# Other places in the plan of a hybrid decoder layer: norms, recurrence, cache loads of the samples and dense steps

## The chip, the cores and the metric

The kernel runs on one core of a Trainium2 chip. The metric is the device time of one execution in microseconds (us), shorter is better. The core has five instruction queues that are in order each and wait for one another by semaphores: TensorE (PE; its weight loads are PEld), VectorE (DVE), ScalarE (ACT), GpSimd (POOL) and SyncE (SP), which here issues all DMA transfers.

## What is computed

One layer of a decoder on 2048 prompt tokens and on 64 sample tokens (8 sequences of 8), cut to what matters here:

```
h = rmsnorm(x)
z = h @ W_in      # q, k, v, indexer q/k/w, GLA q/k/v/r, gate
A = sparse attention: score[t,s] = sum_h w[t,h] * relu(iq[t,h] . ik[s]);
    each query keeps its 256 best keys; softmax(q.k / 8 + bias) over those; @ v
G = gated linear attention in chunks of 64 (a recurrence over the prompt), norm, swish gate
x = x + concat(A, G) @ W_out
x = x + W_down(silu(W_gate h2) * (W_up h2)),  h2 = rmsnorm(x)
y = rmsnorm(x)
```

The samples do the same against a paged cache of 512 keys each and keep 130 keys. The 256 best keys are found by rounds: MAX8 gives the eight largest of a row, MATCH_REPLACE8 takes them out, and 32 rounds make 256 (17 rounds for the samples).

## The kernel before

The prompt goes through in 8 blocks of 256 tokens. Tokens stand in columns, features in partitions. Every dense product takes its weights as two fp16 halves (high and low) and the activations too, and runs three matmuls (L763, L764, L765) in place of one.

The order of the work on all five queues is one list, `PLAN` (function `plan`). Each engine goes through the whole list and does its own part of every step, so a step's place in the list is its place in every queue. For block b the list holds, between three kinds of places:

- **The head of block b**, from the barrier before `PR` to the next: `PR` (norm of the input), the output products `O` of block b-1, `YS` and `YR` (square and scale of the final norm of block b-2, then its store), `XF` (load of the residual of block b-1 and its sum with the `O` products), the 13 input products `P` of block b (25 in block 0), and between these, as the tables `E_NARROW` and `E_WIDE` say (the number is the `P` step behind which a step stands), the index key norm and the gates (`E1` to `E5`), the recurrence (`GA`, `GC`, `GD1`, `GD2`), and `FS` and `FR` (square and scale of the second norm of block b-1). Then the first `HEAD_USES` steps `U` (gate and up products of block b-1), then a barrier.
- **The attention of block b**: index scores `I`, 32 picking rounds `K` for the first 128 queries, `KE`, the rounds for the second 128 queries, and 16 units `A` (2 x 8 heads: logits, softmax, transposes, values). The rest of the `U` steps and the first six of the eight `D` (down products, 66 matmuls each) of block b-1 are spread over this by `interleaved`: it gives each attention step a weight and puts a dense step wherever the share of dense weight done falls behind the share of attention weight passed. The weights are estimates written in `attention_steps`.
- In block 1 the samples' own attention stands ahead of that: `IS0` (which also issues the cache loads), eight `IS` (index scores), 17 rounds `KS`, eight `AS`.

A `U` step of a narrow block holds two weight tiles of 128x1024 and 48 matmuls of 256 columns; the 320-column blocks (b = 1 for `U` and `D`, b = 0 for `P`) have one tile a step.

**Weights.** Six ring slots hold the split tiles. In the first two blocks that use a tile, it is loaded raw, and ACT (`highs`, L1137) and DVE (`lows`, L1429) split it; one of the two blocks writes the halves back to DRAM (L642), and later blocks load them ready (L635). Within a step these stand ahead of the step's own work, and on SP the loads follow the list too:

```
if kind in ("P", "O", "U", "D"):          # SP
    for n in tiles_in(at):
        if n + 5 < len(TILE):
            load(n + 5)
def highs_ahead(at):                      # ACT; DVE's lows_ahead is alike
    for n in tiles_in(at):
        for m in range(5) if n == 0 else [n + 4]:
            if m < len(TILE):
                highs(m)
```

So SP is five tiles ahead of the step that TensorE is to do, and ACT and DVE four. `SP` waits at `YR` for DVE's `y_done` before it stores y (L743), and at the samples' `IS0` for the barrier before it issues one load for the indicator rows, 32 for the index keys (L648), one for the bias, and 12 for keys and values; each of the 44 reads a page number from SBUF first. All dense steps alternate between two PSUM banks, which are released by the evacuation by ACT (`gr`, `gk`, `gq`, `gv`, `v`, `O`, `U`, `D`) or by DVE (`k`, `iq`, `q`, L1565 to L1584).

Of the kernel before, what the change touches and what calls it, by code (L numbers as in the profile page):

```python
# [144 lines left out]
def o_uses(b):  # L145
    return [[t] for t in range(KT)] if b == 1 else [[t, t + 1] for t in range(0, KT, 2)]
# [7 lines left out]
def tiles_of(b):  # L154
    return (2 * b, 2 * b + 1)


E_NARROW = {1: ["E1"], 2: ["E2", "FS"], 3: ["E3", "FR"], 4: ["E4"], 5: ["E5"], 6: ["GA"], 7: ["GC0"], 8: ["GC1", "OUTP"],
            10: ["GD1"], 12: ["GD2"]}
E_WIDE = {3: ["E1"], 5: ["E2"], 6: ["E3"], 9: ["E4"], 10: ["E5"], 11: ["GA"], 12: ["GC0"], 13: ["GC1", "OUTP"],  # L160
          14: ["GSA"], 15: ["GSB"], 16: ["GSN0", "GSN1"], 17: ["GSN2", "GSN3"], 18: ["GSN4", "GSN5"],
          19: ["GSN6", "GSN7"], 22: ["GD1"], 24: ["GD2"]}
HEAD_USES = 4
D_TAIL = 2


def attention_steps(b):

    out = []
    if b == 1:  # L170
        out.append((("IS0", b), 3.0))
        out += [(("IS", b, s), 1.0) for s in range(DB)]
        out.append((("IS9", b), 1.0))
        out += [(("KS", b, r), 1.3) for r in range(ROUNDS_S)]
        out.append((("AS0", b), 2.0))
        out += [(("AS", b, s), 3.0) for s in range(DB)]
        out.append((("AS9", b), 1.0))
        out.append((("BAR", b), 0.5))
    i0, i1 = tiles_of(b)

    def pick(i, r):
        return ("K", b, i, r), 2 * 128 * (i + 1) / 960.0 + 0.3

    def unit(i):
        keys = 128 * (i + 1)
        return max(0.3, keys * 1.6e-3 + 1.2 - keys * 0.84e-3 - (i + 1) * 0.22)

    if b:
# [4 lines left out]
        out.append((("KE", b, i0), 0.5))  # L193
        late = [pick(i1, r) for r in range(ROUNDS)]
    else:
# [40 lines left out]
def plan():  # L236
    steps = [("START", 0), ("PQ", 0)]
    for b in range(NBLK):
# [5 lines left out]
        if b:  # L244
            steps += [("O", b - 1, k) for k in range(len(o_uses(b - 1)))]
            if b >= 2:
                steps += [("YS", b - 2), ("YR", b - 2)]
            steps.append(("XF", b - 1))
# [131 lines left out]
def layer(nc, a):  # L380
    with ExitStack() as ctx:
# [226 lines left out]
        def _(sp):  # L608
# [42 lines left out]
            for at, step in enumerate(PLAN):  # L651
# [38 lines left out]
                if kind == "XF":  # L690
                    if b == 0:
                        for who in ENG:
                            sp.wait_ge(S("bar_" + who), BARS[at - 2 - len(o_uses(0))] + 1)
                    else:
                        sp.wait_ge(S("y_done"), b)
# [22 lines left out]
                if kind == "GD1" and b == NBLK - 1:  # L718
                    sp.wait_ge(S("g_state"), 4 * NBLK)
                    sp.dma_start(a["o_gp"], state[:, :, :]).then_inc(S("outputs"), 16)  # L720
                    outs += 16
                if kind == "IS0":
                    for who in ENG:
# [1323 lines left out]
```

## Time and profile before

| what | value |
|---|---|
| median of 3 runs | 4444.63 us (4441.96 to 4448.02) |
| the profiled execution's own time | 4443.38 us |
| its span, first to last instruction | 4441.6 us |
| PE busy | 3334.8 us, 75% |
| DVE busy | 2531.8 us, 57% |
| ACT busy | 1192.0 us, 27% |
| POOL busy | 1077.5 us, 24% |
| DMA queue q1 | 509.88 MB, 35.3% of 16 engines |
| chain that ended last | PE 29%, DVE 19%, issue 18%, DVE's sequencer 15% |

No engine is busy throughout. Three quarters for TensorE is an average over stages with different limits, so the profile has to be read stage by stage: the head of a block, and its attention. Times in a timeline are counted from the start of the span. PEclk is the share of the full TensorE clock that was granted.

### The profile page before, as it was taken

To read this page: it belongs to the slowest core of one execution; us is meant where nothing else is said; L and a number is where in the kernel's file an instruction comes from. 1 tells how busy PE (TensorE), PEld (TensorE's weight loads), DVE (VectorE), ACT (ScalarE), POOL (GpSimd) and SP (SyncE) were. 2 spreads that over 40 slices of the span, in tenths; PEclk is the share of its full clock that TensorE was granted. 3 is DMA by queue.
4 is the path that set the end of the run, shared out by engine and by line. 5 is a ranking of instruction groups with operands and counts; after the bars stand their busy time and mean duration, and the time that the engine had idled before them with its cause. 6 is when DMAs were issued, how large, how long until landed. Compare 5 with 4: busy or idle time off the path is not lost.

```text
span 4441.6 us, 67462 instructions
## 1 busy us (share of the span) xinstructions
PE 3334.8 (75%) x26714; PEld 2689.3 (61%) x26714; DVE 2531.8 (57%) x4016; ACT 1192.0 (27%) x2002; POOL 1077.5 (24%) x979
## 2 busy tenths in 40 slices
PE   6867477778987878888677957879657889167687
PEld 3656245666666767676566646666546676156577
DVE  3537158645852397238953498534997247996100
ACT  2334123333323221323132301333112324012211
POOL 0233113123612332133112222122310123010142
PEclk8978678789998989999798978889878899678889
DMA  4335344344634433243214332143312143011244
GB/s 155 117 126 186 100 129 144 119 154 137 230 127 140 131 122 125 96 150 125 78 56 152 113 105 85 49 148 108 124 59 66 62 165 125 32 60 52 86 148 147
DMA packets 200573, 514.20 MB, mean 116 GB/s; under 512 B 20242, under 2 KB 79458, under 8 KB 200130
## 3 DMA queue, kind: packets, MB, share of 16 engines
q1 hardware_dynamic: 200258, 509.88, 35.3%
q8 instruction: 212, 3.47, 0.3%
q14 instruction: 103, 0.84, 0.1%
HBM read 443.67 MB, written 66.15 MB: 115 GB/s over the span
## 4 chain that ended last, share of the span: by engine, by line
PE 29%; DVE 19%; issue 18%; DVEq 15%; POOLq 7%; ACT 4%; POOL 3%; DMA 2%; SPq 1%; ACTq 0%
DVEq L1442 11%; DVE top L1439 10%; PE bank L763 6%; PE bank L764 6%; PE bank L765 6%; PE bank L812 3%; DVE T L1462 2%; ACT T L1362 2%; DVEq L1440 2%; PE bank L801 1%; POOLq L1793 1%; DMA FR<-in_xT 1%; DVE T L1441 1%; DVE ring L1429 1%; PE bank L788 1%
## 5 line engine op out<-in xcount | busy, mean ns | idle before, releaser
L763 PE MATMUL bank<-FR,ring 128*128 128x256 f16 (+1 forms) x4224 | 1199.2, 284 | 42.5 <-DVE ring L1429 23.9
L764 PE MATMUL bank<-FR,ring 128*128 128x256 f16 (+1 forms) x4224 | 1197.5, 284 | 0.0
L765 PE MATMUL bank<-FR,ring 128*128 128x256 f16 (+1 forms) x4224 | 1195.3, 283 | 0.0
L1439 DVE MAX8 top<-T 128x8 f32<-128x384 f32 (+14 forms) x465 | 651.7, 1402 | 34.0 <-POOL T L1933 4.2
L1441 DVE MATCH_REPLACE8 T<-top,T 128x384 f32<-128x384 f32 (+14 forms) x465 | 644.2, 1385 | 1.2 <-issue 1.2
L788 PE MATMUL bank<-kT,q 128*128 128x256 f16 (+3 forms) x384 | 134.7, 353 | 513.4 <-DVE mx L1462 489.6
L763 PEld LDWEIGHTS bank<-FR,ring 128*128 128x128 f16 x4224 | 428.6, 101 | 121.8 <-issue 20.0
L764 PEld LDWEIGHTS bank<-FR,ring 128*128 128x128 f16 x4224 | 425.2, 101 | 74.5 <-issue 1.7
L765 PEld LDWEIGHTS bank<-FR,ring 128*128 128x128 f16 x4224 | 425.1, 101 | 73.8
L788 PEld LDWEIGHTS bank<-kT,q 128*128 128x128 f16 x384 | 44.0, 115 | 588.8 <-DVE mx L1462 552.6
L763 PE MATMUL bank<-T,ring 128*128 128x256 f16 (+3 forms) x1280 | 372.9, 291 | 35.0 <-DMA ring<-halves_kept 17.5
L812 PE MATMUL bank<-vtok,T 128*128 128x64 f32 x2176 | 341.4, 306 | 75.6 <-DVE T L1475 56.6
L1462 DVE CUSTOM_DVE_ANT_0 T<-bank,T 128x256 f32<-128x256 f32 (+3 forms) x384 | 194.0, 534 | 339.3 <-PE bank L790 238.9
L812 PEld LDWEIGHTS bank<-vtok,T 128*128 128x128 f32 x2176 | 326.5, 227 | 95.9 <-issue 53.8
L764 PE MATMUL bank<-T,ring 128*128 128x256 f16 (+3 forms) x1280 | 371.6, 290 | 0.0
L765 PE MATMUL bank<-T,ring 128*128 128x256 f16 (+3 forms) x1280 | 370.3, 289 | 0.0
L1409 DVE TENSOR_TENSOR T<-T 128x256 f32<-128x256 f32 (+1 forms) x32 | 13.8, 432 | 606.7 <-ACT T L1121 606.7
L1159 ACT ACTIVATE T<-bank 128x512 f32<-128x512 f32 (+3 forms) x320 | 165.1, 528 | 423.5 <-PE bank L801 423.4
L1150 ACT ACTIVATE T<-T,nmax 128x128 f32<-128x128 f32 (+15 forms) x128 | 153.1, 1196 | 439.0 <-DVE nmax L1465 439.0
L1910 POOL TENSOR_TENSOR ev<-ev 128x512 f32<-128x512 f32 (+1 forms) x99 | 121.9, 1231 | 451.3 <-ACT ev L1336 448.5
L801 PE MATMUL bank<-cst,T 128*128 128x128 f32 x1088 | 205.3, 313 | 18.5 <-ACT T L1150 18.4
L1905 POOL TENSOR_TENSOR ev<-ev 128x512 f32<-128x512 f32 (+1 forms) x99 | 121.5, 1227 | 367.7 <-ACT ev L1334 367.1
(285 smaller groups left out, 5622.4 us busy)
## 6 DMA issues: line engine op xcount, KB each, us to landing
ring<-halves_kept SPq DMA_DIRECT2D x605, 512.0 KB, 3.5
halves_kept<-ring SPq DMA_DIRECT2D x93, 512.0 KB, 5.1
ring<-halves_kept SPq DMA_DIRECT2D x52, 384.0 KB, 3.4
kT<-in_w_gu SPq DMA_DIRECT2D x33, 512.0 KB, 6.1
kT<-in_w_in SPq DMA_DIRECT2D x18, 512.0 KB, 6.7
ikT<-in_w_gu SPq DMA_DIRECT2D x17, 512.0 KB, 5.9
T<-in_xT SPq DMA_DIRECT2D x8, 1024.0 KB, 6.8
FR<-in_xT SPq DMA_DIRECT2D x8, 1024.0 KB, 8.4
```

What stands on the lines that cost most here:

```text
L763: mm(o, lhs[0], rhs[0], start=first, stop=False)
L764: mm(o, lhs[0], rhs[1], start=False, stop=False)
L765: return mm(o, lhs[1], rhs[0], start=False, stop=last)
L788: mm(bank[2 + n % 2][:, 0:kn], q[:, h, cq:cq + 128], kT[:, h // 4, 0, k0:k0 + kn], start=True, stop=False)
L801: last = nc.tensor.transpose(bank[4 + n % 2][:, 128 * (t % 4):128 * (t % 4) + 128], lg[:, u % 2, 128 * t:128 * t + 128], ident)
L812: last = mm(bank[6 + u % 2][:, 0:64], pT[:, GN[i, h, g] % 3, t % 4, :], vtok[:, t, e:e + 64], start=(t == 0), stop=(t == i))
L1150: A(lg[:, u % 2, 0:128 * (i + 1)], lg[:, u % 2, 0:128 * (i + 1)], ACT.Exp, bias=nmax[:, u % 2:u % 2 + 1], accum_out=den[:, u % 4:u % 4 + 1 ...
L1159: A(pT[:, m % 3, 0:w, :], bank[4 + n % 2][:, 0:128 * w].rearrange("p (t n) -> p t n", n=128), ACT.Copy).then_inc(S("a_pTc"), 1)
L1439: v.max(top8[rows, :], view)
L1441: v.match_replace(view, top8[rows, :], view, TAKEN)
L1442: dve.drain()
L1462: v.tensor_tensor_reduce(lg[:, u % 2, k0:k0 + kn], bank[2 + n % 2][:, 0:kn], m, 1.0 / Q_SCALE, OUTSIDE, ALU.add, ALU.max, mx[:, u % 2, c:c ...
```

## The change

It moves steps in the list and adds one step, `LOADS`, which has only SP's part of the former `IS0`. No arithmetic and no transfer is added or taken away.

```
-E_NARROW = {1: ["E1"], 2: ["E2", "FS"], 3: ["E3", "FR"], 4: ["E4"], 5: ["E5"], 6: ["GA"], 7: ["GC0"], 8: ["GC1", "OUTP"],
-            10: ["GD1"], 12: ["GD2"]}
+E_NARROW = {1: ["E1"], 2: ["E2"], 3: ["E3", "FS"], 4: ["E4"], 5: ["E5", "FR"], 8: ["GA"], 9: ["GC0"], 10: ["GC1", "OUTP"],
+            11: ["GD1"], 12: ["GD2"]}
-E_WIDE = {3: ["E1"], 5: ["E2"], 6: ["E3"], 9: ["E4"], 10: ["E5"], 11: ["GA"], ...
+E_WIDE = {3: ["E1"], 5: ["E2"], 7: ["E3"], 9: ["E4"], 11: ["E5"], 13: ["GA"], ...
...
-HEAD_USES = 4
+HEAD_USES = 6
...
-        out.append((("IS0", b), 3.0))
-        out += [(("IS", b, s), 1.0) for s in range(DB)]
+        out.append((("LOADS", b), 60.0))
+        out.append((("IS0", b), 5.0))
+        out += [(("IS", b, s), 1.5) for s in range(DB)]
...
-        out += [(("AS", b, s), 3.0) for s in range(DB)]
+        out += [(("AS", b, s), 5.0) for s in range(DB)]
...
-        return max(0.3, keys * 1.6e-3 + 1.2 - keys * 0.84e-3 - (i + 1) * 0.22)
+        return max(0.3, 2.5 - keys * 1e-3)
...
-        late = [pick(i1, r) for r in range(ROUNDS)]
+        late = [(step, w - 0.4) for step, w in (pick(i1, r) for r in range(ROUNDS))]
...
-            steps += [("O", b - 1, k) for k in range(len(o_uses(b - 1)))]
+            uses = [("O", b - 1, k) for k in range(len(o_uses(b - 1)))]
+            half = len(uses) // 2
             if b >= 2:
-                steps += [("YS", b - 2), ("YR", b - 2)]
+                steps += [("YS", b - 2)] + uses[:half] + [("YR", b - 2)] + uses[half:]
+            else:
+                steps += uses
...
-                if kind == "IS0":
+                if kind == "LOADS":
```

In `E_WIDE`, `GD1` goes from 22 to 23, the recurrence of the samples by two places, and `GD2` stays at 24. The `XF` wait of block 0 is written by another index and names the same barrier. Four lines come in ahead of the engines' code, so that a line of the code before stands four lines further down now (L1348 is L1352).

The list itself changes in this way (narrow blocks, b of 3 to 7): `PR O O O O YS YR XF P...` becomes `PR YS O O YR O O XF P...`; `FS` stands one and `FR` two `P` steps later, `GA` and `GC` two, `GD1` one. Two `U` steps leave the attention for the head. In block 1, four `U` steps stand in the attention ahead of the index scores of the prompt that were behind them: before, 1 `U` step stood between the barrier and `IS` 0 and 11 between the barrier and the end of the samples' part; now 7 and 14, of which six stand between `LOADS` and `IS0`. In the attention of blocks 1 to 4 the last spread `D` steps move behind the last picking round: one in blocks 1, 3 and 4, two in block 2. In blocks 5 to 7 they stay ahead of it.

**ACT in the first instructions behind the barrier of block 1's samples.** L1333 and L1334, L1336 are the evacuations of a `U` pair, L1137 the high halves of the tiles ahead, L1366 `IS0`, L1372 and L1373 `IS`. Before:

```order
L1366 ACTIVATE T<-bank 64x512
L1137 ACTIVATE ring<-ikT 128x1024
L1137 ACTIVATE ring<-kT 128x1024
L1333 ACTIVATE ev<-bank 128x512
L1334 ACTIVATE ev<-bank 128x512
L1372 ACTIVATE T<-bank 64x512
L1373 ACTIVATE T<-bank 64x64
```

The same place now (L1141 is the high half, L1337 and L1338, L1340 the evacuations, L1370 `IS0`), from the fourth `U` step behind `LOADS` on:

```order
L1141 ACTIVATE ring<-kT 128x1024
L1141 ACTIVATE ring<-vtok 128x1024
L1340 ACTIVATE ev<-bank 128x512
L1141 ACTIVATE ring<-ikT 128x1024
L1141 ACTIVATE ring<-kT 128x1024
L1337 ACTIVATE ev<-bank 128x512
L1338 ACTIVATE ev<-bank 128x512
L1141 ACTIVATE ring<-kT 128x1024
L1141 ACTIVATE ring<-vtok 128x1024
L1340 ACTIVATE ev<-bank 128x512
L1370 ACTIVATE T<-bank 64x512
L1141 ACTIVATE ring<-ikT 128x1024
```

`IS0` stood ahead of the first `U` step and stands behind six of them now, with their twelve splits.

**DVE in the head of block 6.** L1524 to L1531 are `FR`, L1409 to L1415 a Newton step of a norm, L1615 to L1625 `E4`, L1637 and L1638 `E5`, L1565 the evacuation of the seventh `P` step. Before:

```order
L1524 SCALAR_TENSOR_TENSOR FR<-FR,gvec,T 128x256 x4
L1529 CAST FR<-FR 128x1024
L1531 TENSOR_TENSOR FR<-FR 128x1024
L1409 TENSOR_TENSOR T<-T 128x256
L1411 TENSOR_TENSOR T<-T 128x256
L1413 TENSOR_SCALAR T<-T 128x256
L1415 TENSOR_TENSOR T<-T 128x256
L1615 TENSOR_TENSOR T<-T 128x256
L1619 TENSOR_SCALAR ik<-T,gates 128x256
L1623 TENSOR_SCALAR ikT<-ik 128x256
L1625 SCALAR_TENSOR_TENSOR ikT<-ik,ikT 128x256
L1637 TENSOR_TENSOR T<-T 64x2x256
```

The same queue now, from the end of `E5` on:

```order
L1642 TENSOR_TENSOR T<-T 64x2x256
L1413 TENSOR_TENSOR T<-T 128x256
L1415 TENSOR_TENSOR T<-T 128x256
L1417 TENSOR_SCALAR T<-T 128x256
L1419 TENSOR_TENSOR T<-T 128x256
L1528 SCALAR_TENSOR_TENSOR FR<-FR,gvec,T 128x256 x4
L1533 CAST FR<-FR 128x1024
L1535 TENSOR_TENSOR FR<-FR 128x1024
L1528 SCALAR_TENSOR_TENSOR FR<-FR,gvec,T 128x256 x4
L1533 CAST FR<-FR 128x1024
L1535 TENSOR_TENSOR FR<-FR 128x1024
L1569 TENSOR_SCALAR k<-bank 128x512
```

`FR` stood ahead of `E4` and `E5`; now it stands behind both and directly ahead of the evacuation of the seventh `P` step.

## Rows read from the trace of the kernel before

**Rows 1.** Busy time by stretch: stretch, length, busy (count) by engine, PEclk, DMA.

```profile
451.00:679.00 228.00, 141.43 (x905) 93.17 (x906) 82.67 (x156) 47.71 (x89) 31.18 (x27) 0.71 0.38 118
679.00:892.00 213.00, 156.57 (x1137) 128.24 (x1136) 159.04 (x358) 72.67 (x126) 55.95 (x53) 0.82 0.41 134
...
1068.00:1374.00 306.00, 272.45 (x1889) 198.53 (x1889) 199.31 (x368) 101.24 (x202) 113.63 (x133) 0.93 0.46 156
...
2908.00:3072.00 164.00, 136.19 (x1274) 118.18 (x1274) 58.14 (x103) 46.04 (x66) 49.28 (x36) 0.91 0.45 150
3072.00:3513.00 441.00, 313.40 (x2304) 245.78 (x2304) 341.27 (x434) 113.45 (x203) 75.30 (x78) 0.84 0.22 71
```

**Rows 2.** Waits of TensorE, head of block 6 (2908:3072): total, times, longest us.

```profile
PE bank L780 <- POOL FR L1791: 9.7, 2, 7.2
PE bank L929 <- DVE T L1638: 9.3, 1, 9.3
...
PE bank L763 <- DMA ring<-halves_kept: 1.3, 1, 1.3
```

**Rows 3.** Timeline of GpSimd, same head: start, length, instruction, idle before.

```profile
2932.32 4.62 POOL L1791 TENSOR_TENSOR FR<-FR 128x1024 f32<-128x1024 f32 x3 [21.63 <-ACT FR L1348]
```

**Rows 4.** Timeline of SP, same head: the store of y.

```profile
2947.49 0.59 SPq L743 DMA_DIRECT2D o_y<-FR  x1
```

**Rows 5.** Timeline of VectorE, same head: begin of `FR`, begin of `E4`.

```profile
2974.07 0.43 DVE L1409 TENSOR_TENSOR T<-T 128x256 f32<-128x256 f32 x1 [9.42 <-ACT T L1121]
...
2983.28 0.42 DVE L1409 TENSOR_TENSOR T<-T 128x256 f32<-128x256 f32 x1
```

**Rows 6.** Timeline of GpSimd, same head: begin of `GD2`, of two `U` pairs.

```profile
3042.61 1.89 POOL L1779 TENSOR_TENSOR T<-T 128x1024 f32<-128x1024 f32 x1 [47.58 <-ACT T L1304]
...
3059.89 1.27 POOL L1905 TENSOR_TENSOR ev<-ev 128x512 f32<-128x512 f32 x1
...
3065.97 1.27 POOL L1905 TENSOR_TENSOR ev<-ev 128x512 f32<-128x512 f32 x1
```

**Rows 7.** Timeline of ScalarE, same head: an evacuation of a `U` step.

```profile
3062.65 0.60 ACT L1333 ACTIVATE ev<-bank 128x512 f32<-128x512 f32 x1 [4.64 <-PE bank L765]
```

**Rows 8.** Waits of TensorE, head of block 2 (892:1068).

```profile
PE bank L1045 <- POOLq L562: 12.3, 1, 12.3
PE bank L929 <- DVE T L1638: 11.0, 1, 11.0
PE bank L780 <- POOL FR L1791: 10.0, 2, 7.0
PE bank L763 <- DMA ring<-halves_kept: 4.5, 1, 4.5
```

**Rows 9.** Timeline of SP behind the barrier of block 1.

```profile
450.75 0.51 SPq L726 DMA_DIRECT2D T<-in_rep  x1
...
490.14 12.43 SPq L648 DMA_DIRECT2D T<-in_cache  x12
```

**Rows 10.** Timeline of ScalarE, its first row behind those loads.

```profile
507.70 1.06 ACT L1137 ACTIVATE ring<-kT 128x1024 f16<-128x1024 f32 x1 [49.24 <-DMA kT<-in_w_gu]
```

**Rows 11.** Timeline of VectorE: first round `KS`, first split behind it.

```profile
541.85 0.76 DVE L1439 MAX8 top<-T 64x8 f32<-64x582 f32 x1 [0.82 <-ACT T L1376]
...
554.80 1.23 DVE L1429 SCALAR_TENSOR_TENSOR ring<-kT,ring 128x1024 f16<-128x1024 f32 x1 [10.00 <-ACT ring L1137]
```

**Rows 12.** Timeline of GpSimd, head of block 1: beside VectorE's splits, and without.

```profile
436.56 2.06 POOL L1907 TENSOR_TENSOR ev<-ev 128x512 f32<-128x512 f32 x1
...
445.83 1.26 POOL L1907 TENSOR_TENSOR ev<-ev 128x512 f32<-128x512 f32 x1
```

**Rows 13.** Groups of VectorE, block 1's picking (679:832): busy us, mean ns.

```profile
L1429 DVE SCALAR_TENSOR_TENSOR ring<-vtok,ring 128x1024 f16<-128x1024 f32 (+1 forms) x7 | 10.4, 1485 | 0.1
```

**Rows 14.** Waits of TensorE, block 0 (80:240).

```profile
PE bank L922 <- DVE T L1593: 8.2, 1, 8.2
PE bank L929 <- DVE FR L1638: 5.1, 1, 5.1
```

More of the change, by code:

```diff
@@ L155, in tiles_of @@
     return (2 * b, 2 * b + 1)
-E_NARROW = {1: ["E1"], 2: ["E2", "FS"], 3: ["E3", "FR"], 4: ["E4"], 5: ["E5"], 6: ["GA"], 7: ["GC0"], 8: ["GC1", "OUTP"],
-            10: ["GD1"], 12: ["GD2"]}
-E_WIDE = {3: ["E1"], 5: ["E2"], 6: ["E3"], 9: ["E4"], 10: ["E5"], 11: ["GA"], 12: ["GC0"], 13: ["GC1", "OUTP"],
-          14: ["GSA"], 15: ["GSB"], 16: ["GSN0", "GSN1"], 17: ["GSN2", "GSN3"], 18: ["GSN4", "GSN5"],
-          19: ["GSN6", "GSN7"], 22: ["GD1"], 24: ["GD2"]}
-HEAD_USES = 4
+E_NARROW = {1: ["E1"], 2: ["E2"], 3: ["E3", "FS"], 4: ["E4"], 5: ["E5", "FR"], 8: ["GA"], 9: ["GC0"], 10: ["GC1", "OUTP"],
+            11: ["GD1"], 12: ["GD2"]}
+E_WIDE = {3: ["E1"], 5: ["E2"], 7: ["E3"], 9: ["E4"], 11: ["E5"], 13: ["GA"], 14: ["GC0"], 15: ["GC1", "OUTP"],
+          16: ["GSA"], 17: ["GSB"], 18: ["GSN0", "GSN1"], 19: ["GSN2", "GSN3"], 20: ["GSN4", "GSN5"],
+          21: ["GSN6", "GSN7"], 23: ["GD1"], 24: ["GD2"]}
+HEAD_USES = 6
 D_TAIL = 2
@@ L692, in _ @@
                         for who in ENG:
-                            sp.wait_ge(S("bar_" + who), BARS[at - 2 - len(o_uses(0))] + 1)
+                            sp.wait_ge(S("bar_" + who), BARS[AT["PR", 1] - 1] + 1)
                     else:
```

## The prediction, made before the changed kernel was run

> **What bounds the kernel now.** The page first: TensorE is busy 75% of the span, VectorE 57%, and the chain that ended last has shares of both, so there is no single bound. The view by stretches divides it [rows 1]. In the head of a block (164 us in block 6) TensorE is busy 136 us, VectorE 58: TensorE sets the pace, and 28 us are waits. In the attention from block 3 on VectorE is the bound: 341 of 441 us in block 6, most of it picking, with TensorE's dense steps lying beside it. Block 2's attention has the wide dense steps and is TensorE's: 272 of 306 us. Block 1 is neither: in the samples' part (451 to 679) nobody is busy over 62%, in the prompt's part (679 to 892) VectorE is at 159 of 213 us, because it splits raw weights as well as picking.
>
> The waits of TensorE in a head come next [rows 2, 8]. Three go to the norms: `YR`'s sum (7.2 us in block 6), the weights held back by SP's wait for y (1.3 here, 4.5 in block 2), `FR`'s sum (9.7 less 7.2, so 2.5). The fourth is `GA`, 9.3 and 11.0 us, waiting for `E5` on VectorE, which stood behind `FR`. A head ends on GpSimd: `GD2` starts at 3042.61, the two `U` pairs at 3059.89 and 3065.97 [rows 6], so a pair costs 6.1 us and the barrier opens at 3072.1. In block 2 TensorE waits 12.3 us for that [rows 8]. A `U` step costs TensorE 5.2 us (4.64 us of waiting plus 0.60 of evacuation) [rows 7]; a narrow `D` step has 66 matmuls against 48, so 7.2.
>
> All durations are of the profiled execution, 4443.4 us in all (span 4441.6); the median is 1.2 us more.
>
> **Heads of blocks 2 to 7.** I follow block 6, whose head begins at 2908. `YS` now stands ahead of the `O` steps. ScalarE is free 5 us in, squares for 2 us (the sum on GpSimd started 21.6 us after its last work, because ScalarE first had to evacuate four `O` steps), the sum takes 4.6 us alone [rows 3] and would be done 11.5 us in, when two `O` steps of 5.3 us have just ended. But VectorE now scales the input (`PR`) at that very time. Beside VectorE's splits a GpSimd add took 2.06 us in place of 1.26 [rows 12]; at that ratio the sum takes 7.6 us. So `YR`'s wait is between 0 and 3.5 us; I take 1.5. y is stored 10.6 us after its sum (the sum at 2936.9, the store at 2947.49 [rows 3, 4]), so about 24 us in, against 39 now. SP waits there, and has loaded only up to the first half of the first `P` step. TensorE arrives at the second half about 29 us in and the tile lands behind 1 MB of y: a wait of 1 to 5 us, I take 2.6 (before, 1.3). `FR`'s sum comes one `P` step later: 1.8 us left of 2.5. `GA`'s wait goes whole, since `E4` and `E5` are no longer behind `FR`. In its place: `FR` takes VectorE 9.2 us [rows 5] directly ahead of the evacuation of the seventh `P` step, which frees the bank of the ninth. I get 4.3 us of a new wait there, bounds 0 and 9.2. Sum: old waits 20.3, new 10.2, and 2.6 us less at the half clock behind the long wait: 12.7 us won at `GA`. Of this `GD1` gives back one `P` step, 5.2, since it stands behind the twelfth now; and the barrier one more pair on GpSimd, 6.1 us, as three `U` pairs follow `GD2` instead of two. Left: 1.4 us, with two more `U` steps done. So the waits go, and the tail takes nearly all. By the same steps blocks 4 and 7 give 2, block 6 2, blocks 3 and 5 (longer waits before) 5 each. Block 2: 25.5 us of waits besides the barrier [rows 8], new ones some 10, clock 5, so 21 won, 5.2 and 4.4 (a narrower pair) given back: 11. Heads together: 27 us less. Bounds 5 and 45: each of the six can be 3 us off on either side.
>
> The Trainium skill, page "SBUF — State Buffer", section "SBUF: two separate sides", says that VectorE and GpSimd share a port pair as an exclusive lock, so that the loser blocks for the whole instruction. The two GpSimd rows agree in direction, 2.06 against 1.26 us [rows 12]. By the lock the moved sum could last its own 4.6 us plus all of `PR`'s 7.4, done 19 us in, and `YR`'s wait would be the old one; the six heads would then give some 30 us less.
>
> **The two `U` steps that leave the attention.** From block 3 on they lay beside picking on VectorE and cost nothing there, so nothing comes back: value 0, bounds 0 and 2 a block. In block 2 TensorE is the bound, so two wide steps (3.3 us each) come back, and two `D` steps fill a wait behind the last picking round: 9.5 us less. Block 3's last `U` among the index scores moves behind them: 1.5 less.
>
> **`D` steps behind the last round.** In blocks 3 and 4 one `D` (7.2 us) moves from under the picking, where TensorE had room, into the last units, where TensorE is the bound. Two times 6.7 us more, 3 us back because the logits of the units before are less late: 10.5 more. Bounds 3 and 15.
>
> **Block 0.** `E3` one step later takes 4 of its 8.2 us wait, the later `GA` all 5.1 [rows 14]; `GD1` stands one step later, 3.4 us. 6 us less, bounds 0 and 10.
>
> **Block 1.** This is the largest term, and it goes the other way.
> Head: its waits go as above, but VectorE's splits run beside GpSimd to the end, so a third `U` pair takes 8 to 10 us, and the head ends 9 us later.
> Samples: SP issues the 44 cache loads from 450.75 to 502.6 [rows 9], and no weight meanwhile. In the kernel before ScalarE got its next raw tile at 507.70, after 49.2 us of waiting [rows 10], and TensorE could do one `U` step ahead of that. Now six `U` steps stand between `LOADS` and `IS0`, but SP's queue still has all 44 loads ahead of the third one's weights. So TensorE does two (10.5 us), waits some 46 us, and only then does the other four, 5.3 us each at least; then `IS0` must go through GpSimd, VectorE and ScalarE with TensorE idle for 8 to 12 us, then `IS` with two `U` steps among them. The first round `KS` stood 91 us behind the barrier (541.85 [rows 11]); I get 133. `KS` then has two `U` steps among it in place of four and loses part of the 10 us wait for a split [rows 11]: 32 us for 51. `AS` is the same but for its last `U` step. So the samples' part ends 20 us later, with three more `U` steps done.
> Prompt: five fewer dense steps, 13 fewer splits at 1.4 us [rows 13], so 18 us off VectorE, and 5 of its waits; a `U` step now stands among the index scores (5.5 more) and a `D` with its splits behind the last round (8 more). 10 us less.
> Block 1 together: 19 us more. Bounds: 5 less (everything that leaves the prompt's part comes back at its pace there, 10 us a step, for half the steps) and 45 more (nothing comes back, and the four steps run at 7.8 us).
>
> **Sum.** -27 (heads) -9.5 (block 2) -1.5 (block 3) +10.5 (`D`) -6 (block 0) +19 (block 1) = -14.5 us: 4428.9 for the profiled execution, 4430 beside the median. `KS`, `K` and the products are the same instructions; the last block's end is untouched.
>
> **Rivals.**
> (a) Block 1 gives its time back. The prompt's part is bound by VectorE's splits and picking; if `U` steps there cost what they seem to, 10 us each, five fewer make up for the samples, and the total is -35 to -45: 4400. For it: VectorE at 159 of 213 us [rows 1]. Against it: the rounds stay, only the splits go.
> (b) The heads give nothing. GpSimd ends each head with three pairs in place of two, and if its sums are slowed as by the lock above, blocks 3 to 7 are level and block 2 gives 5: -27 becomes -5, the sum +7.5, so 4452 at the far end, 4443 if half of it. For it: the barrier already waited for GpSimd in every head [rows 6, 8]. Against it: at least 12 us of waits per head go first.
> (c) Slower: the queue of SP in block 1. The six `U` steps behind `LOADS` are starved by the 44 loads; the price is the stretch from barrier to `KS`, and it decides from 45 us (the 43.5 of the heads, block 2 and 0, less the `D` steps' 10.5, plus the 9 that can be told). At 50 us of loss in block 1 the total is +17: 4461. For it: 49.2 us of waiting for a raw tile [rows 10], which no step of the change shortens. Against it: work done before need not be done later.
> (d) That nothing happens, because all is off the path: +-5 us. Against it the barrier waits above. Counted with (b).
>
> **Chances.** Forecast (4415 to 4437) 0.45; (a) 0.17; (b) and (d) 0.20; (c) 0.18. About 0.2%, 9 us, is what a measurement of this kernel can tell from no change. Below 4435.7: (a), most of the forecast, 0.57. Within: 0.26. Above 4453.5: 0.17. Range: 4400 to 4462, from (a) to (c).
>
> **What would show it.** In the heads TensorE's wait at `GA` is gone, one of 2 to 6 us is there at the ninth `P` step, and three `U` pairs stand behind `GD2` on GpSimd. In block 1 TensorE waits over 40 us for a raw tile within 15 us of the barrier, `IS0`'s first matmul comes some 90 us behind it, and the prompt's part is about 10 us shorter. The prediction is wrong if `GA` still waits, if the heads end over 6 us earlier each, or if the samples' part is no longer than before.

## The result, and the profile after

The changed kernel takes 4491.36 us (median of 4 runs, 4488.87 to 4514.35) against 4443.3 us (median of 4, 4438.3 to 4448.02): ratio 1.012, interval 1.0085 to 1.0155. It is slower by 48 us where 4430 was predicted. The profiled execution has a span of 4490.3 us, 48.7 more than before.

The same stretches as in [rows 1], read from the changed kernel (stretch, length, busy time and count by engine, PEclk, DMA): head and samples' part of block 1; its prompt's part; head of block 2; attention of blocks 2, 3 and 4; head and attention of block 6.

```profile
270.90:699.30 428.40, 294.19 (x2416) 230.06 (x2416) 196.45 (x285) 129.03 (x194) 108.21 (x75) 0.81 0.49 157
699.30:903.20 203.90, 125.48 (x896) 101.60 (x896) 142.72 (x348) 59.93 (x109) 32.20 (x37) 0.76 0.28 94
903.20:1071.10 167.90, 136.04 (x1227) 110.00 (x1228) 77.44 (x109) 53.00 (x79) 55.92 (x45) 0.93 0.50 167
1071.10:1386.10 315.00, 272.49 (x1840) 195.59 (x1841) 199.70 (x368) 99.41 (x199) 109.81 (x128) 0.91 0.46 151
1557.40:1859.90 302.50, 233.49 (x1824) 193.19 (x1824) 205.30 (x370) 72.69 (x136) 69.20 (x72) 0.87 0.30 97
2028.80:2384.50 355.70, 262.14 (x1953) 210.57 (x1953) 251.31 (x386) 86.56 (x168) 69.49 (x73) 0.85 0.26 82
2944.60:3114.20 169.60, 143.17 (x1370) 124.65 (x1371) 63.58 (x103) 47.30 (x69) 54.06 (x41) 0.94 0.48 157
3114.20:3557.20 443.00, 295.08 (x2208) 231.12 (x2209) 341.33 (x434) 112.25 (x200) 69.75 (x72) 0.83 0.21 66
```

The same stages of the kernel before, for the comparison (block 1 in its two parts, attention of block 4):

```profile
280.50:678.90 398.40, 276.01 (x2177) 209.66 (x2178) 184.84 (x275) 114.66 (x177) 86.26 (x60) 0.79 0.45 146
678.90:891.80 212.90, 156.47 (x1137) 128.13 (x1137) 159.04 (x358) 72.67 (x126) 55.76 (x53) 0.82 0.41 133
2000.50:2344.50 344.00, 260.89 (x2048) 211.06 (x2048) 251.71 (x386) 88.35 (x171) 75.42 (x77) 0.90 0.29 91
```

Block 1's first part is 30 us longer, its second 9 shorter. The head of block 6 has 96 matmuls more than before (two `U` steps) and is 5.4 us longer; the attention behind it has 96 fewer and is 2.3 us longer. Stage by stage (attention of block 7 without its last two `D` steps, which both kernels have):

| stages | before | after | difference | predicted |
|---|---|---|---|---|
| block 0 | 262.3 | 252.9 | -9.4 | -6 |
| block 1 | 611.3 | 632.3 | +21.0 | +19 |
| heads of blocks 2 to 7 | 1004.9 | 1015.0 | +10.1 | -27 |
| attention of block 2 | 305.8 | 315.0 | +9.2 | -9.5 |
| attention of blocks 3 and 4 | 637.4 | 658.2 | +20.8 | +9 |
| attention of blocks 5 to 7 | 1311.9 | 1309.0 | -2.9 | 0 |

Where the head's time went is in its waits. Waits of TensorE in the head of block 6 of the changed kernel (engine, line, what it waited for: us, times, longest):

```profile
PE bank L767 <- DVE kT L1574: 7.9, 1, 7.9
PE bank L767 <- DMA ring<-halves_kept: 6.2, 1, 6.2
...
PE bank L1012 <- ACT T L1296: 1.8, 1, 1.8
PE bank L784 <- POOL FR L1795: 1.7, 2, 1.4
```

Against [rows 2]: `GA` no longer waits, `YR`'s sum 0.3 us, `FS`'s 1.4. The wait for the weights behind y is 6.2 us where it was 1.3, and a new one of 7.9 stands at the ninth `P` step. With the 0.3, the 1.4 and the 1.8 at `GD1` these are 17.6 us, where 20.3 stood before. In both long waits the moved sums have a part, which VectorE's and GpSimd's timelines show together. VectorE at the scaling of the input (`PR`, L1513), then at the begin of `E4` (L1619 and L1623):

```profile
2951.51 5.18 DVE L1513 SCALAR_TENSOR_TENSOR T<-T,gvec 128x256 f32<-128x256 f32 x4
...
2958.68 1.67 DVE L1513 SCALAR_TENSOR_TENSOR T<-T,gvec 128x256 f32<-128x256 f32 x4
...
3004.95 2.61 DVE L1619 TENSOR_TENSOR T<-T 128x256 f32<-128x256 f32 x1
3007.64 1.20 DVE L1623 TENSOR_SCALAR ik<-T,gates 128x256 f32<-128x256 f32 x1
```

GpSimd, the sum of `YS` in the same head:

```profile
2951.39 4.62 POOL L1795 TENSOR_TENSOR FR<-FR 128x1024 f32<-128x1024 f32 x3 [4.26 <-ACT FR L1352]
```

And the first of these rows of `E4` in the kernel before, where no sum lay beside it:

```profile
2985.14 0.42 DVE L1615 TENSOR_TENSOR T<-T 128x256 f32<-128x256 f32 x1
2985.64 0.41 DVE L1619 TENSOR_SCALAR ik<-T,gates 128x256 f32<-128x256 f32 x1
```

Four scalings take 5.18 us while GpSimd's sum runs and 1.67 when it is over; an addition of 0.42 us takes 2.61 beside `FS`'s sum. GpSimd keeps its 4.62 us. So these moved sums were not slowed, as I had taken; they hold VectorE up by 3.5 us each. `E4` goes on in `L1627` and `L1629` to 3010.20, so 5.25 us in all for 1.80 before. All six heads have both holds: the four scalings take 5.2 to 6.2 us for 1.7, `E4` 5.25 to 6.25 for 1.8.

The kernel before had the same already. In the head of block 1, beside the GpSimd addition of [rows 12] that took 2.06 us for 1.26, VectorE's split takes 2.29 us, where one alone takes 1.23 [rows 11]. In the head of block 6 `E5`'s second addition takes 1.74 us beside one of GpSimd, its first 0.68:

```profile
435.21 2.29 DVE L1429 SCALAR_TENSOR_TENSOR ring<-ikT,ring 128x1024 f16<-128x1024 f32 x1
...
2989.39 0.68 DVE L1637 TENSOR_TENSOR T<-T 64x512 f32<-64x512 f32 x1 [2.46 <-ACT T L1264]
2990.00 1.74 DVE L1638 TENSOR_TENSOR T<-T 64x512 f32<-64x512 f32 x1
```

The first hold goes on through ScalarE, which needs the scaled tiles' buffer for `YR`'s root. The root begins 4.4 us behind the sum's end, where it was 1.3 before, so 3.1 us are lost there:

```profile
2960.44 0.47 ACT L1121 ACTIVATE T<-bank,cst 128x256 f32<-128x256 f32 x1 [4.04 <-DVE T L1513]
```

So y is stored at 2969.68 (SP's timeline), 25.1 us into the head, and SP, which had issued three weight tiles ahead of it, issues the next at 2970.39. TensorE has waited for that tile since 26.6 us into the head when it lands (last row, PE's timeline):

```profile
2947.94 5.56 SPq L639 DMA_DIRECT2D ring<-halves_kept  x3
2969.68 0.59 SPq L747 DMA_DIRECT2D o_y<-FR  x1
2970.39 3.55 SPq L639 DMA_DIRECT2D ring<-halves_kept  x4
...
2977.47 0.39 PE L767 MATMUL bank<-T,ring 128*128 128x256 f16 x1 [6.22 <-DMA ring<-halves_kept]
```

Then the end of the head, on GpSimd: the Newton steps behind `GD1`, and three `U` pairs behind `GD2`.

```profile
3078.36 1.90 POOL L1783 TENSOR_TENSOR T<-T 128x1024 f32<-128x1024 f32 x1 [60.04 <-ACT T L1308]
...
3095.62 1.27 POOL L1909 TENSOR_TENSOR ev<-ev 128x512 f32<-128x512 f32 x1
...
3101.71 1.27 POOL L1909 TENSOR_TENSOR ev<-ev 128x512 f32<-128x512 f32 x1
...
3107.80 1.26 POOL L1909 TENSOR_TENSOR ev<-ev 128x512 f32<-128x512 f32 x1
```

The chain starts 133.8 us into the head; in [rows 6] it started 134.4 us in (3042.61 less 2908.2). All that the norms' move won is 0.6 us there, and the third pair takes 6.1: together the 5.4 us that the head is longer, to 0.1.

In block 1 the prediction's picture came out as drawn. ScalarE behind the barrier:

```profile
452.89 1.06 ACT L1141 ACTIVATE ring<-ikT 128x1024 f16<-128x1024 f32 x1 [8.39 <-POOLq L566]
509.92 1.06 ACT L1141 ACTIVATE ring<-kT 128x1024 f16<-128x1024 f32 x1 [55.98 <-DMA kT<-in_w_gu]
```

ScalarE waits 55.98 us for a raw tile and TensorE 47.1 us for ScalarE (TensorE's waits from 452 to 560):

```profile
PE bank L767 <- ACT ev L1338: 47.1, 1, 47.1
PE bank L767 <- POOLq L566: 13.1, 1, 13.1
PE bank L1055 <- DVE T L1724: 8.5, 1, 8.5
```

The third is `IS0`'s, and `IS0` starts at 544.1, 91 us behind the barrier (90 had been forecast). The block's head is 11.5 us longer, the samples' part 18.5 longer and the prompt's part 9 shorter, for 9, 20 and 10 in the forecast.

### The profile page after: what moved, and what is told of

The parts are those of the page before. It is cut to its first block, busy times and chain, and to the rows that moved or that the text cites. A ratio compares the mean times of both kernels' runs of the same rounds, so it can differ in the third digit from the quotient of the medians.

```text
span 4490.3 us, 67462 instructions
## 1 busy us (share of the span) xinstructions
PE 3320.2 (74%) x26714; PEld 2681.8 (60%) x26714; DVE 2555.9 (57%) x4016; ACT 1191.7 (27%) x2002; POOL 1071.8 (24%) x979
## 4 chain that ended last, share of the span: by engine, by line
PE 33%; DVE 23%; DVEq 17%; issue 11%; POOLq 5%; ACT 5%; POOL 2%; DMA 2%; SPq 1%; ACTq 0%
DVEq L1446 13%; DVE top L1443 11%; PE bank L767 8%; PE bank L768 7%; PE bank L769 7%; PE bank L816 3%; DVEq L1444 2%; DVE T L1466 2%; DVE ring L1433 1%; ACT T L1366 1%; PE bank L805 1%; DVE T L1445 1%; PE bank L792 1%; POOLq L1915 1%; POOLq L1912 1%
## 5 line engine op out<-in xcount | busy, mean ns | idle before, releaser
L767 PE MATMUL bank<-FR,ring 128*128 128x256 f16 (+1 forms) x4224 | 1198.5, 284 | 89.3 <-ACT ev L1338 47.1
L792 PEld LDWEIGHTS bank<-kT,q 128*128 128x128 f16 x384 | 44.1, 115 | 677.1 <-DVE mx L1466 637.4
L1413 DVE TENSOR_TENSOR T<-T 128x256 f32<-128x256 f32 (+1 forms) x32 | 14.9, 466 | 455.2 <-ACT T L1125 455.0
L1923 POOL TENSOR_TENSOR FR<-FR,ev 128x256 f32<-128x256 f32 (+1 forms) x64 | 49.8, 778 | 762.9 <-ACT ev L1349 762.9
L1909 POOL TENSOR_TENSOR ev<-ev 128x512 f32<-128x512 f32 (+1 forms) x99 | 120.6, 1218 | 431.6 <-ACT ev L1338 431.2
```

The lines of the kernel that those rows point to most:

```text
L767: mm(o, lhs[0], rhs[0], start=first, stop=False)
L792: mm(bank[2 + n % 2][:, 0:kn], q[:, h, cq:cq + 128], kT[:, h // 4, 0, k0:k0 + kn], start=True, stop=False)
```

## The experiments

Blocks' times below are from each kernel's own profile, cut at the same steps; medians are of its runs, with the kernel before on the same chip beside them. Each edit is against the changed kernel or against another experiment, as said. The ratios are the recorded ones and not quotients of the two medians. The experiments ran on three chips, on which the kernel before has medians of 4441.81 (e1 to e4), 4439.97 (e5 to e8) and 4444.33 (e9 to e12).

A stretch "from the last round on" is cut at `KE`, the step behind it. How many of the spread `D` steps stand behind the last round decides several experiments, and the list of the steps gives it (before, then changed): 1 and 1 in block 1, 1 and 2 in block 2, 0 and 1 in blocks 3, 4 and 5, none in 6 and 7. So block 2 has one more there, not two, block 1 none, and block 5 has one directly ahead of `KE`. e1 and e9 have 3, 2, 1 and 1 in blocks 2 to 5, and of these one directly ahead of `KE` in blocks 2, 3 and 5.

**Two `U` steps fewer in the heads of blocks 2 to 7.**

```
-            steps += [s for s, _ in u[:HEAD_USES]]
+            steps += [s for s, _ in u[:HEAD_USES.get(b, 4)]]
-HEAD_USES = 6
+HEAD_USES = {1: 6}
```

> The changed kernel with four U steps instead of six between GD2 and the barrier of blocks 2 to 7 (block 1 keeps six); the two that leave go back among the picking rounds. Theory 1 (a head is bound by TensorE and ends on GpSimd, so its last two U steps cost the pair of 6 us there, while among the rounds they lie beside VectorE and are free; and TensorE, having more to do among the rounds, keeps its clock longer): heads 2 to 7 are each 5 to 6 us shorter, attention of blocks 3 to 7 the same or up to 5 us shorter, total 4455 (clock no matter) down to 4440. Rival (work is work: what leaves the head is paid in the attention): attention grows by 5 us a block, total 4485 to 4495.

4476.24 us (before 4441.81; ratio 1.0083, 1.0066 to 1.01). The six heads take 983.8 us for 1015.0, 5.2 each. The attention of blocks 2 to 7 takes 2292.7 for 2282.2: a third of it is paid there. The total lies between the two forecasts: theory 1 for the heads, with a part of the rival behind them. The pair on GpSimd was the price.

**The old weights of rounds and units in blocks 2 to 7.**

```
     def unit(i):
         keys = 128 * (i + 1)
+        if b != 1:
+            return max(0.3, keys * 1.6e-3 + 1.2 - keys * 0.84e-3 - (i + 1) * 0.22)
         return max(0.3, 2.5 - keys * 1e-3)
 ...
-        late = [(step, w - 0.4) for step, w in (pick(i1, r) for r in range(ROUNDS))]
+        late = [(step, w - (0.0 if b != 1 else 0.4)) for step, w in (pick(i1, r) for r in range(ROUNDS))]
```

> The changed kernel with the weights of the picking rounds and units as before for blocks 2 to 7, so that no D step but the last two stands behind the last picking round. Theory 1 (a D step behind the last round costs its full 7 to 9 us in blocks 2, 3 and 4, and is free under the rounds): the tails of blocks 2, 3 and 4 are 7, 8 and 9 us shorter, nothing else moves, total 4467. Rival (the step costs the same under the rounds, since the chain through TensorE's logits is as late there): the stretches under the rounds grow by what the tails lose, total 4485 to 4492.

4503.54 us (before 4441.81; ratio 1.014, 1.0118 to 1.0162), 12 above the change in the medians, which the two intervals don't tell apart. Block 4 does what theory 1 says, from its last round on (the kernel after, then this one):

```profile
2291.70:2384.50 92.80, 75.92 (x553) 62.60 (x553) 22.18 (x88) 31.67 (x59) 14.62 (x18) 0.89 0.18 56
```

```profile
2310.00:2393.10 83.10, 65.54 (x487) 53.80 (x487) 21.70 (x88) 31.18 (x58) 13.93 (x17) 0.92 0.16 51
```

66 matmuls fewer, 9.7 us less. But in block 2, where a `D` step stands between the last round and `KE`, the stretch of the second tile's rounds up to `KE` grows from 121.1 to 135.5 us (to the end of the last round 126.7), and in block 3 from 110.0 to 118.4. VectorE waits 40.3 us there for 27.6 in block 2, of these 33.0 for splits of ScalarE, and 20.8 for 12.4 in block 3, of these 14.9 for logits of TensorE. The attention of blocks 5 to 7, whose weights the edit also changes, is 10 us longer. So theory 1 holds for one block and falls as a sum.

**Block 1 as before** (its norms, four `U` steps in its head, cache loads directly ahead of `IS0`, old weights; `E_ONE` is the old `E_NARROW`).

```
-        out.append((("LOADS", b), 60.0))
-        out.append((("IS0", b), 5.0))
+        out.append((("LOADS", b), 0.0))
+        out.append((("IS0", b), 3.0))
 ...
-        after = E_NARROW if b else E_WIDE
+        after = (E_ONE if b == 1 else E_NARROW) if b else E_WIDE
```

> The changed kernel with block 1 as before: norms of its head, four U steps in it, the cache loads directly ahead of IS0 with the sample steps' old weights, the prompt's picking with the old dense steps. Theory 1 (the six U steps put between the cache loads and IS0 starve behind 44 loads in SP's queue, and only part of the lost time comes back in the prompt's picking): block 1 is 21 us shorter, the rest the same, total 4470. Rival (block 1's loss is the price of moved work, and other blocks change with it, since the clock is granted on what TensorE did before): total 4480 or more, with the heads and block 2 slower by 10 us.

4474.9 us (before 4441.81; ratio 1.0084, 1.0056 to 1.0112). Block 1 takes 611.4 us for 632.3, as before the change (611.3), and every head and attention behind it is within 2 us of the change's. Block 1's 21 us are its own. Its time alone spreads: in the nine traces with the old steps in it, it takes 598.3 to 611.4 us (median 608.9), in the four with the new ones 625.6 to 632.6 (median 630.4).

**Norms alone**: the kernel before with the new places of norms and recurrence in block 0 and in the heads of blocks 2 to 7, and nothing else.

```
-                steps += [("YS", b - 2), ("YR", b - 2)]
+                steps += [("YS", b - 2)] + uses[:half] + [("YR", b - 2)] + uses[half:]
 ...
-E_NARROW = {..., 2: ["E2", "FS"], 3: ["E3", "FR"], ..., 6: ["GA"], 7: ["GC0"], 8: ["GC1", "OUTP"], 10: ["GD1"], ...}
+E_NARROW = {..., 3: ["E3", "FS"], ..., 5: ["E5", "FR"], 8: ["GA"], 9: ["GC0"], 10: ["GC1", "OUTP"], 11: ["GD1"], ...}
```

> The kernel before with only the norms and the recurrence at the new places in the heads of blocks 2 to 7 and of block 0 (YS ahead of the O steps, YR in their middle, FS and FR one P step later, GA behind the ninth P step, GD1 behind the twelfth); four U steps, block 1 and all weights as before. Theory 1 (moving the norms wins 5 us of waits in a head of blocks 3 to 7, some 13 in block 2 and 9 in block 0, and what ate it was the two U steps, D and block 1): block 0 9 us shorter, head 2 12 us, heads 3 to 7 1 to 4 us each, attention as in the kernel before, total 4400 to 4415. Rival (GpSimd's sums now lie beside VectorE's scaling and hold it up, so the norms' own places cost what they save): heads 2 to 7 the same as before or longer, total 4434 to 4445.

4423.24 us (before 4441.81; ratio 0.995, 0.9932 to 0.9967). The heads take 980.9 us for 1004.9: 13.3 less in block 2, 0.5 longer to 5.7 shorter in the others. The move is worth something where the waits were long (block 2, and 3 and 5), and nothing in block 6. The total lies between theory 1 (up to 4415) and the rival (from 4434), nearer to theory 1.

**`FR` and `GA` at better places**, against the kernel of the norms alone.

```
-E_NARROW = {..., 5: ["E5", "FR"], 8: ["GA"], 9: ["GC0"], 10: ["GC1", "OUTP"], 11: ["GD1"], 12: ["GD2"]}
+E_NARROW = {..., 5: ["E5"], 6: ["FR"], 7: ["GA"], 8: ["GC0"], 9: ["GC1", "OUTP"], 10: ["GD1"], 12: ["GD2"]}
```

> The kernel of e4 (norms alone moved) with the places behind E5 changed in blocks 2 to 7: FR behind the evacuation of the seventh P step instead of ahead of it, and GA, GC0, GC1, GD1 behind the eighth, ninth, tenth and eleventh P step instead of the ninth to twelfth. Theory 1 (the 7.9 us wait at the ninth P step is FR's scaling ahead of one evacuation, and the head ends on GpSimd's chain GD1, newton, GD2, two U pairs, so one P step earlier is one P step won): GD1 on TensorE comes some 8 us earlier, head of block 6 from 164.7 to 157 us, seven per cent less waiting, total 45 us less than e4, about 4380. Rival (FR on VectorE costs TensorE the same wait at whatever place, and the barrier waits for TensorE by then): heads within 2 us of e4's, total 4415 to 4425.

4367.26 us (before 4439.97; ratio 0.9846, 0.9815 to 0.9878): 56 us less than e4 by the medians, 46 by the ratios, and 124 less than the change. The six heads take 927.9 us for 980.9, so nearly all of it is theirs. Head of block 6, e4 and then e5:

```profile
2889.60:3054.30 164.70, 133.94 (x1275) 115.76 (x1276) 63.03 (x103) 45.59 (x66) 48.44 (x36) 0.91 0.45 149
```

```profile
2838.00:2993.00 155.00, 134.64 (x1274) 117.75 (x1274) 62.25 (x103) 45.70 (x66) 48.50 (x36) 0.92 0.48 158
```

TensorE does the same in it. The Newton steps on GpSimd now start 125.3 us into the head for 133.8:

```profile
2963.26 1.89 POOL L1787 TENSOR_TENSOR T<-T 128x1024 f32<-128x1024 f32 x1 [50.80 <-ACT T L1312]
```

The wait at the ninth `P` step is gone; one of 6.5 stands at `GC0`, and 6.2 for the weights behind y. Theory 1, and more than it. The two holds of VectorE are there as before (5.19 and 5.26 us in this head): what is gone is what waited behind the second.

**`YR` behind all `O` steps**, against e4; **and both edits**.

```
-                steps += [("YS", b - 2)] + uses[:half] + [("YR", b - 2)] + uses[half:]
+                steps += [("YS", b - 2)] + uses + [("YR", b - 2)]
```

> The kernel of e4 with YR behind all O steps (YS stays ahead of them), so that SP has loaded five weight tiles more when it stands waiting to store y. Theory 1 (the 6.2 us wait at the second half of the first P step is SP's wait for y): that wait falls to 1 to 2 us and everything behind it in the head, GpSimd's end too, comes 4 to 5 us earlier: heads 2 to 7 each 4 to 5 us, total 4395. Rival (the input of the residual arrives later with it and FS takes the place of the wait, or the tile is late because 1 MB of y is being written at the same time): heads within 2 us of e4's, 4415 to 4425.

> The edits of e5 and e6 together. Theory 1 (both waits are separate and both stand ahead of GpSimd's chain): the gains add up, head of block 6 some 152 us, total 4355 to 4370. Rival (TensorE's own work of 126 us at full clock plus the barrier's remains, and the second edit only moves a wait): no better than the better of the two.

4419.69 us alone (ratio 0.995, 0.9932 to 0.9968) and 4365.84 with the edit of e5 (ratio 0.9841, 0.9819 to 0.9863), before 4439.97 in both. The wait for weights falls from 6.2 to 3.6 us, not to 1 or 2, and head 6 from 164.7 to 160.9. But block 2's head, with eight `O` steps ahead of `YR`, is 10 us longer in both, which takes the gain of the others: the total doesn't move. Alone that is the rival's total (4415 to 4425); together, 4365.84 lies in the range of both theories. e7 is the fastest profile of the study, with e5 and e10 within 3 us in the medians, less than the runs tell apart.

**TensorE given idle matmuls**: the changed kernel, with the first matmul of a tile issued again in the `U` steps of the attention of blocks 2 to 4.

```
-            def columns(o, n, halves_of, kn, k0=0, of=None):
+            def columns(o, n, halves_of, kn, k0=0, of=None, again=0):
 ...
+                for _ in range(again):
+                    mm(o, w[0][:, 0:o.shape[0]], halves_of(k0)[0], start=True, stop=True)
                 for k in range(kn):
 ...
+                                again={1: 2, 2: 3, 3: 3}.get(b, 0) if step[2] >= HEAD_USES else 0
```

> The changed kernel with TensorE given back, as idle repetition, the matmuls that left the attention of blocks 2 to 4: in each of their U steps among index scores and rounds the first matmul of a tile is issued two (block 2) or three times more, each a closed group of its own, 76 in block 2 and 96 in blocks 3 and 4, some 10 us a block at full clock. The result is the same. Theory 1 (the attention of blocks 2 to 4 got 9 to 12 us longer because TensorE, with fewer steps there, was granted the lower clock for 15, 32 and 38 us more): the time at the lower clock falls back towards 42, 44 and 72 us and the attention of the three blocks shrinks by 3 to 10 us each although TensorE does more; total 4470 to 4485. Rival (the longer attention comes from where the D steps stand, and from nothing of the clock): the three attentions are as long or up to 10 us longer, total 4490 to 4510.

4515.36 us (before 4439.97; ratio 1.0167, 1.0141 to 1.0194). The three attentions take 315.0, 306.8 and 358.9 us for 315.0, 302.5 and 355.7, and PEclk in blocks 3 and 4 (the two rows) is 0.88 and 0.86, for 0.87 and 0.85:

```profile
1569.10:1875.90 306.80, 247.99 (x1921) 206.57 (x1921) 205.29 (x370) 72.79 (x136) 69.10 (x73) 0.88 0.30 95
2044.00:2402.90 358.90, 272.75 (x2048) 220.19 (x2049) 251.32 (x386) 86.56 (x168) 69.34 (x73) 0.86 0.26 81
```

Theory 1's forecast, shorter attentions, falls; the rival's comes. But the clock came back in part: time at 1.2 GHz is 44, 76 and 100 us in the three for 57, 76 and 110, where the kernel before has 42, 44 and 72. So the run shows that such filling wins nothing. What the lower clock costs there it does not tell apart, since it adds work at the same time.

**A `D` step behind the last round, alone**: e5 with the change's weights.

> The kernel of e5 with the change's weights for rounds and units in blocks 2 to 7 (four U steps in the heads, block 1 as before): one more D step behind the last round in block 2, one in block 3, one in block 4, none in blocks 5 to 7. Theory 1 (such a D step costs its whole 7 us where VectorE's rounds do not cover it): behind the last round block 4 takes 9 us more, blocks 2 and 3 6 to 8 each, and the rounds of these blocks get no shorter, total 20 us above e5, some 4387. Rival (what leaves the rounds comes back there, as it did in block 2 of e2): total within 8 us of e5.

Its edit is the one of e2 taken back. 4384.46 us (before 4444.33; ratio 0.9857, 0.9829 to 0.9885), 17 above e5 in the medians, on another chip, which the two intervals don't tell apart. From the last round on block 2 takes 90.3 us for 79.8, block 3 84.6 for 80.7, block 4 90.8 for 83.5, and the rounds give nothing like it back: those of the second tile are 1.0 us shorter in block 3 and 3.3 longer in block 4, and in block 2 5 longer up to `KE`, with the `D` step ahead of it, and 1.6 shorter to the end of the last round. Over all traces, the stretch from `KE` on takes 82.9 to 83.6 us in block 4 without a `D` step (86.9 in e10) and 90.8 to 92.9 with one; in block 2 79.8 to 85.2 with one behind `KE` and 88.9 to 93.0 with two; in block 3 73.1 to 80.8 and 80.4 to 84.6. So theory 1 is shown for block 4, and for block 2 in direction; for block 3 the two ranges meet.

**Two `U` steps in a head for four**, against e5 (`HEAD_USES.get(b, 2)`).

> The kernel of e5 with two U steps instead of four between GD2 and the barrier of blocks 2 to 7. Theory 1 (a head ends on GpSimd: the chain GD1, newton, GD2, then 6.1 us a pair, so one pair less is 5 to 6 us; and among the rounds of blocks 3 to 7 two U steps more cost at most 2 us): heads 5 to 6 us shorter each, block 2's attention 6 longer, the others 0 to 2 longer, total 4335 to 4350. Rival (the end of the head is TensorE's now that the waits are gone, or the attention pays for what leaves, as it half did in e1): total 4360 to 4370.

4364.57 us (before 4444.33; ratio 0.9818, 0.979 to 0.9845). The heads give 37.1 us, 6.2 each, and the attention takes 28.3 back: 9.2 in block 3, 10.9 in block 4, where VectorE now waits 23.3 and 18.9 us in the second tile's rounds, for 11.2 and 8.4. So the heads do as theory 1 says, and the sum goes to the rival.

**The new places in block 1's head too**, against e5.

> The kernel of e5 with its places behind E1 to GD2 in the head of block 1 too. Theory 1 (GA's wait of 10.5 us there goes as in the other heads, since FR stands behind E5): that wait is gone and block 1's head 5 to 10 us shorter, total 5 to 10 us below e5. Rival (VectorE splits raw weights there to the end of the head, so FR's scaling delays a split in place of GA and TensorE waits as long for the ring): block 1 within 3 us of e5.

The edit drops `E_ONE`. 4374.31 us (before 4444.33; ratio 0.9827, 0.9802 to 0.9853). `GA`'s wait of 10.5 us is gone, 7.9 at `GC0` and 3.3 for an evacuation have come; block 1 takes 608.1 us for 605.3, within the spread of equal steps that stands at e3. The rival is right, though not by the ring.

**`YS` in the middle of the `O` steps**, against e7.

```
-                steps += [("YS", b - 2)] + uses + [("YR", b - 2)]
+                steps += uses[:half] + [("YS", b - 2)] + uses[half:] + [("YR", b - 2)]
```

> The kernel of e7 with YS between the second and the third O step instead of ahead of the first. Theory 1 (VectorE's scalings of PR, 1.7 us for four before and 5.2 after the change, each ended with one of GpSimd's three additions of YS's sum: the two engines take turns, and VectorE is the one that waits): with the sum some 6 us later the first four scalings take 1.7 us again, whatever VectorE does while the sum runs is stretched instead, and the head is no longer. Rival (the scalings are slow for another reason, such as what lies in the buffers): they take 5 us again. The total stays within 10 us of e7, 4366.

4369.64 us (before 4444.33; ratio 0.9826, 0.9799 to 0.9853). VectorE's scalings in head 6, then GpSimd's sum:

```profile
2864.04 1.67 DVE L1517 SCALAR_TENSOR_TENSOR T<-T,gvec 128x256 f32<-128x256 f32 x4
```

```profile
2870.81 5.13 POOL L1799 TENSOR_TENSOR FR<-FR 128x1024 f32<-128x1024 f32 x3 [11.15 <-ACT FR L1356]
```

1.67 us again, with the sum behind them, as in all six heads. Theory 1 in this. Nothing of VectorE is stretched in return: its last addition (1.22 us) had begun 0.59 us ahead of the sum, and it is GpSimd's 5.13 us that are 0.5 longer than the 4.62. Head 6 takes 149.7 us in both, the six together 923.8 for 917.9: with `YR` behind all `O` steps nothing waited for the scalings.

## Why the prediction was wrong

The sum was -14.5 us and came out as +48.7, 63 off: 37 in the heads, 19 in block 2, 12 in blocks 3 and 4, the rest within 4 us each.

- **Heads of blocks 2 to 7: the step that failed.** "Sum: old waits 20.3, new 10.2": the new ones are 17.6. Half of the difference is at the ninth `P` step, 7.9 us for 4.3. The reading behind it was wrong: that where a sum on GpSimd lies beside VectorE, the sum is slowed, and VectorE not. `FS`'s sum holds `E4` up by 3.45 us, and `E5`, `FR` and the evacuation stand behind it; without them the wait would be 4.4. At y the same reading cost little: the store came 25.1 us into the head for "about 24", since the root lost 3.1 us where I had given the sum 3.0. But `YR` and the weights behind y take 0.3 + 6.2 us for 1.5 + 2.6, as TensorE stands at that tile 26.6 us into the head and not 29. The 1.8 at `GD1` was not in the sum. So GpSimd's chain starts 0.6 us earlier, where 12.7 less 5.2 had been counted on. e12 shows the hold at `PR`; for `E4` it is read from the trace, and no run takes that one away alone. The section "SBUF: two separate sides" of the page "SBUF — State Buffer" in the Trainium skill, which calls the shared port an exclusive lock, stood in the prediction in a rival, though with GpSimd as the one that waits. The trace agrees with the lock: taken one by one, the first three scalings begin 0.06 to 0.12 us behind one each of GpSimd's three additions and end 0.28 us behind it.
- The tail of a head was right: one `P` step for `GD1`, one pair of 6.1 us on GpSimd, so 5.2 us (e1) to 6.2 (e10) a head. With the waits hardly shorter, it made the heads longer. Rival (b) had the heads at -5; they came to +10.
- **Block 2 and the `D` steps.** -9.5 had two `D` steps "fill a wait behind the last picking round". It is one more than before, and it fills none: TensorE is busy 4.5 us longer there (69.9 for 65.5), and the stretch is 5.8 us longer, 88.9 for 83.1 (10.5 longer in e9 against e5). I took 6.7 us each in blocks 3 and 4 and "3 us back"; block 4 lost 9.7 (e2), block 3 3.9 (e9), and nothing came back. The rest of the +9.2 and +20.8 is in part the trace before, which is the lowest of seven (last section).
- That two `U` steps leaving the rounds bring nothing in blocks 3 to 7 was right for the change: in e1 the two that come back take 6 us in these five blocks together. It is no rule: two more cost 9 and 11 us in blocks 3 and 4 (e10), and in e2 as many with other spacing cost 8 in block 3. What decides, as far as VectorE's waits tell, is whether a dense step stands ahead of logits for which VectorE is about to wait.
- **Block 1** was right in mechanism and size, +21.0 for +19, by e3. Rival (c) had the right place but too large a price (it needed 45 us; the stretch from the barrier to the first round `KS` grew by 35, from 91 to 126), and the right sign for a reason that was elsewhere. Its 43.5 does not come out of the terms either: 27, 9.5, 1.5 and 6 are 44, and with the rest the bound is 42.5. In the heads, six times 3 us on either side of 27 give 9 to 45 and not 5 to 45.
- **Block 0**: -9.4 for -6, but by luck. The waits of 8.2 and 5.1 us are gone; one of 4.6 has come, and the barrier's went from 22.7 to 25.9. What is left is less than the spread that the last section shows.
- The signs that the prediction named came, but for the size at the ninth `P` step; they did not tell 4430 from 4491.

The attentions of blocks 2 and 3 differ by up to 11 and 8 us among kernels whose steps there stand alike, and the granted clock goes with it. Block 2 in e5 and in e11, the shortest and the longest:

```profile
1032.00:1334.10 302.10, 269.67 (x1889) 196.20 (x1889) 199.31 (x368) 101.32 (x202) 112.58 (x133) 0.94 0.47 158
```

```profile
1043.50:1356.80 313.30, 279.96 (x1889) 204.06 (x1889) 199.30 (x368) 101.20 (x202) 113.36 (x133) 0.90 0.45 152
```

TensorE is busy 10.3 us longer for the same matmuls. The change's 315.0 us for 305.8 has to be read beside this spread, so of the 19 us by which block 2 missed its forecast a part can't be told from it. What stays open is why the clock differs: e8's added work gave some of it back and won nothing.

## What to carry to other kernels

Before a step of GpSimd is moved, look at what VectorE does at the new place: either of the two can be the one that waits (GpSimd in [rows 12] and e12, VectorE at `PR` and `E4`), and the price goes on along whatever waits for it. Follow a head to its last engine: only what reaches that chain's start is won, and each item added behind it counts in full. Here `FR` behind one evacuation and `GA` to `GD1` one `P` step earlier gave some 50 us, over twice what the larger edit of the norms had given. A filler under another engine's work is free only while it does not stand ahead of what that engine waits for next.

## What the runs showed of the hardware

Block 0 is the same instructions in the changed kernel and in all twelve experiments, and takes 252.9 to 267.2 us. One of the shortest (e5) and the longest (e10):

```profile
18.10:271.70 253.60, 177.44 (x1305) 130.00 (x1305) 122.02 (x276) 79.57 (x143) 59.29 (x52) 0.83 0.36 117
```

```profile
18.30:285.50 267.20, 191.16 (x1304) 136.24 (x1304) 122.04 (x276) 79.81 (x143) 59.35 (x51) 0.78 0.34 111
```

VectorE, ScalarE and GpSimd are busy as long to 0.3 us; TensorE is busy 13.7 us longer, at a mean granted clock of 0.78 for 0.83. The stretch holds 88 us at 1.2 GHz in one and 117 in the other. So one profile of this stage can't tell 10 us from nothing. The median of the thirteen traces is 262.7 us, and the single trace before has 262.3: there was no gain of 9.4 to measure. The attention of blocks 2 to 4 with the steps as before the change takes 943.2 to 959.4 us in seven traces; the trace before is the lowest of them.
